# Gate and up chunks of the second block: one 512-column product for the high weights, and the two halves of a bank added on VectorE

## What is computed

```python
def swiglu(x, w_gate, w_up, w_down):
    return (jax.nn.silu(x @ w_gate) * (x @ w_up)) @ w_down

for l in range(DEPTH):                     # 2
    x = x + 0.5 * swiglu(rmsnorm(x, ffn1_norm[l]), ffn1_w_gate[l], ffn1_w_up[l], ffn1_w_down[l])
    x = x + hybrid_mixer(rmsnorm(x, mix_norm[l]), ...)
    x = x + 0.5 * swiglu(rmsnorm(x, ffn2_norm[l]), ffn2_w_gate[l], ffn2_w_up[l], ffn2_w_down[l])
```

## Time and profile before

| | before |
|---|---|
| median of 3 runs | 2207.34 us |
| the profiled execution: its own time, its span | 2209.08 us, 2207.3 us |
| TensorE busy, matmuls | 2139.0 us (97%), 17311 |
| VectorE busy | 1497.4 us (68%) |
| ScalarE busy | 1076.1 us (49%) |
| GpSimd busy | 581.6 us (26%) |
| mean DMA rate | 174 GB/s |

### The profile page before, as it was taken

One profiled execution on the slowest core, in us unless ns is written; L12 is line 12 of the kernel. 1 busy time (PEld: TensorE's weight loads), 2 busy tenths in 40 slices (PEclk: granted clock), 3 DMA queues, 4 the chain that ended last, 5 costly groups with the idle time before them and its releaser, 6 DMA issues.

```text
span 2207.3 us, 39976 instructions
## 1 busy us (share of the span) xinstructions
PE 2139.0 (97%) x17311; PEld 2033.7 (92%) x17311; DVE 1497.4 (68%) x1850; ACT 1076.1 (49%) x1432; POOL 581.6 (26%) x280
## 2 busy tenths in 40 slices
PE   7999999999999999999999999999999999999999
PEld 4989899898999888989999999889999999879999
DVE  5977775777678677676666556876556556786555
ACT  3666573433455747543345445554345444555433
POOL 0963315899248260466000000100000000100000
PEclk9999999999999999999999999999999999999999
DMA  9752346677657315566555555335555566434554
GB/s 317 235 170 85 111 127 193 228 261 234 206 169 228 107 39 160 175 197 221 183 191 172 191 191 172 112 99 177 187 191 171 192 191 191 132 98 142 187 189 133
DMA packets 332857, 383.95 MB, mean 174 GB/s; under 512 B 12551, under 2 KB 315402, under 8 KB 332554
## 3 DMA queue, kind: packets, MB, share of 16 engines
q1 hardware_dynamic: 332234, 381.23, 54.0%
q10 hardware_dynamic: 448, 0.16, 0.0%
HBM read 380.32 MB, written 1.05 MB: 173 GB/s over the span
## 4 chain that ended last, share of the span: by engine, by line
PE 74%; DVE 14%; ACT 7%; issue 3%; SPq 1%; DMA 0%; ACTq 0%; DVEq 0%
PE bank L761 16%; PE bank L762 16%; PE bank L763 15%; DVE weights_low L1457 6%; PE bank L1004 5%; PE bank L1003 5%; PE bank L1005 5%; ACT weights_high L2194 4%; DVE arena L1585 2%; PE bank L777 1%; PE bank L1042 1%; PE bank L1239 1%; PE bank L902 1%; PE bank L1224 1%; PE bank L894 1%
## 5 line engine op out<-in xcount | busy, mean ns | idle before, releaser
L1457 DVE TENSOR_TENSOR weights_low<-ring,weights_high 128x2048 fp32r<-128x2048 f32 (+1 forms) x304 | 752.2, 2474 | 429.0 <-ACT weights_high L2194 428.5
L761 PE MATMUL bank<-h_high,weights_high 128*128 128x256 f32 x3296 | 936.5, 284 | 22.6 <-DVE weights_low L1457 16.0
L762 PE MATMUL bank<-h_low,weights_high 128*128 128x256 f32 x3296 | 919.0, 279 | 0.0
L763 PE MATMUL bank<-h_high,weights_low 128*128 128x256 f32 x3296 | 915.8, 278 | 0.0
L2194 ACT ACTIVATE weights_high<-ring 128x2048 fp32r<-128x2048 f32 (+1 forms) x304 | 581.8, 1914 | 683.0 <-PE bank L763 530.2
L761 PEld LDWEIGHTS bank<-h_high,weights_high 128*128 128x128 f32 x3296 | 618.6, 188 | 43.2 <-DVE weights_low L1457 25.2
L762 PEld LDWEIGHTS bank<-h_low,weights_high 128*128 128x128 f32 x3296 | 620.3, 188 | 3.5 <-issue 3.4
L763 PEld LDWEIGHTS bank<-h_high,weights_low 128*128 128x128 f32 x3296 | 617.6, 187 | 0.0
L1003 PE MATMUL bank<-hidden_high,weights_high 128*128 128x256 f32 x1056 | 295.5, 280 | 1.8 <-DVE hidden_low L1723 1.0
L1004 PE MATMUL bank<-hidden_low,weights_high 128*128 128x256 f32 x1056 | 293.9, 278 | 0.0
L1005 PE MATMUL bank<-hidden_high,weights_low 128*128 128x256 f32 x1056 | 293.3, 278 | 0.0
(11 more groups left out here) (441 smaller groups left out, 2821.8 us busy)
## 6 DMA issues: line engine op xcount, KB each, us to landing
ring<-in_w_in SPq DMA_DIRECT2D x80, 1024.0 KB, 5.3
ring<-in_w_up SPq DMA_DIRECT2D x44, 1024.0 KB, 5.4
ring<-in_ffn_w_gate SPq DMA_DIRECT2D x44, 1024.0 KB, 5.4
ring<-in_ffn_w_up SPq DMA_DIRECT2D x44, 1024.0 KB, 5.4
ring<-in_ffn_w_down SPq DMA_DIRECT2D x44, 1024.0 KB, 5.0
side<-in_w_ada SPq DMA_DIRECT2D x42, 1024.0 KB, 7.9
ring<-in_w_down SPq DMA_DIRECT2D x22, 1024.0 KB, 5.0
ring<-in_w_dn_out SPq DMA_DIRECT2D x8, 1024.0 KB, 5.2
```

Source lines behind the costliest of these rows:

```text
L761: mm(o[:, m, :], a_, high[:, t, :], start=(t == 0), stop=False)
L762: mm(o[:, m, :], a_, low[:, t, :], start=False, stop=False)
L763: last = mm(o[:, m, :], b_, high[:, t, :], start=False, stop=(t == KT - 1))
L1457: v.tensor_tensor(low, wide(q), high.bitcast(F32), ALU.subtract).then_inc(chunk_split, 1)
```

## The change

`h_high` and `h_low` become the two halves of one tensor `h_both`, in the order and of the size they had. The gate and up chunks of the second block's four networks go through a new function `linear2`: for each half m and tile t, one product of the high weights with 512 columns (256 of the high input, then 256 of the low input), and one of the low weights with the high input, 256 columns, into the first 256 columns of the same bank. So each half m has a bank of its own: `L[...]` for m = 0, and `B[4]` or `B[5]` for m = 1. On VectorE `add_halves` sums each bank's two halves with one reduction (128 x 512 read, 128 x 256 written to SBUF); `rinv` and the hidden product then read SBUF. Two semaphores, `gate_added` and `up_added`, free the banks.

```diff
-        h_high = sb("h_high", P, KT, T, dt=F32R)
-        h_low = sb("h_low", P, KT, T, dt=F32R)
+        h_both = sb("h_both", P, 2, KT, T, dt=F32R)
+        h_high, h_low = h_both[:, 0], h_both[:, 1]
...
             if kind[0] == "g":
-                return gate_scaled, FP * (fi - 2) + i + 1
+                return gate_added, FP * (fi - 2) + i + 1
+            if kind[0] == "u" and fi >= 2:
+                return up_added, FP * (fi - 2) + i + 1
             return hidden_ready, FP * fi + i + 1
...
+        pair_bank = lambda key: (L[R[key] % 2], B[4 + R[key] % 2])
...
+            def linear2(key, norm=None):
+
+                n = SI[key]
+                wh, wl = WH[n % 2], WL[n % 2]
+                pe.wait_ge(chunk_split, n + 1)
+                pe.wait_ge(*release(PREV[key]))
+                for m in range(2):
+                    o = pair_bank(key)[m]
+                    both = o[:, :].rearrange("p (h t) -> p h t", h=2)
+                    for t in range(KT):
+                        if norm is not None and m == 0:
+                            pe.wait_ge(norm_ready, KT * norm + t + 1)
+                        a_, b_ = wh[:, t, m * P:(m + 1) * P], wl[:, t, m * P:(m + 1) * P]
+                        mm(both, a_, h_both[:, :, t, :], start=(t == 0), stop=(t == KT - 1), skip_group_check=True)
+                        last = mm(o[:, 0:T], b_, h_high[:, t, :], start=False, stop=(t == KT - 1), skip_group_check=True)
+                last.then_inc(chunk_multiplied, 1)
...
             def ffn(ka, kb, kc, l, ni, fi):
                 for i in range(FP + 1):
-                    if i < FP:
+                    if i < FP and ka != "ua":
+                        linear2((ka, l, i), norm=ni if i == 0 else None)
+                        if i == 0:
+                            sum_added(ni)
+                        linear2((kb, l, i))
+                    elif i < FP:
                         linear3((ka, l, i), h_high, h_low, norm=ni if i == 0 else None)
-                        if i == 0 and ni in ADDED:
-                            sum_added(ni)
                         linear3((kb, l, i), h_high, h_low)
...
+            def add_halves(key, dst):
+
+                return [v.tensor_reduce(dst[:, m * T:(m + 1) * T], b[:, :].rearrange("p (h t) -> p t h", h=2), AXX, ALU.add)
+                        for m, b in enumerate(pair_bank(key))]
+
             def hidden(key, fi, i, act, ahead):
 
-                dve.wait_ge(chunk_multiplied, M[key] + 1)
+                if fi < 2:
+                    dve.wait_ge(chunk_multiplied, M[key] + 1)
                 if i >= 2:
                     dve.wait_ge(hidden_ready, FP * fi + i - 1)
-                v.tensor_tensor(HT[:, i % 2, :], act, L[R[key] % 2][:, :], ALU.mult).then_inc(hid_whole, 1)
+                if fi < 2:
+                    v.tensor_tensor(HT[:, i % 2, :], act, L[R[key] % 2][:, :], ALU.mult).then_inc(hid_whole, 1)
+                else:
+                    v.tensor_tensor(HT[:, i % 2, :], act, FB[:, i % 2, :], ALU.mult).then_inc(hid_whole, 1)
...
-                    v.tensor_tensor(fa, LV[R[ka, l, i] % 2], over(rinv[:, :], 2), ALU.mult).then_inc(gate_scaled, 1)
+                    ins = add_halves((ka, l, i), FA[:, i % 2, :])
+                    ins[1].then_inc(gate_added, 1)
+                    then(ins[0])
+                    dve.wait_ge(gate_added, FP * (fi - 2) + i + 1)
+                    v.tensor_tensor(fa, fa, over(rinv[:, :], 2), ALU.mult).then_inc(gate_scaled, 1)
                     split(SI[kb, l, i] + 2)
                     dve.wait_ge(ffn_act, FP * fi + i + 1)
                     then(v.tensor_tensor(fa, fa, over(rinv[:, :], 2), ALU.mult))
+                    dve.wait_ge(chunk_multiplied, M[kb, l, i] + 1)
+                    ins = add_halves((kb, l, i), FB[:, i % 2, :])
+                    ins[1].then_inc(up_added, 1)
+                    then(ins[0])
+                    dve.wait_ge(up_added, FP * (fi - 2) + i + 1)
                     hidden((kb, l, i), fi, i, FA[:, i % 2, :], SI[kb, l, i] + (3 if i else 2))
```

More of the change, by code:

```diff
@@ L424, in build @@
         gate_scaled = sem("gate_scaled")
+        gate_added = sem("gate_added")
+        up_added = sem("up_added")
         squares_ready = sem("squares_ready")
```

## The result

| | before | after |
|---|---|---|
| median of 18 runs each | 2210.93 us (2205.24 to 2215.99) | 2215.82 us (2212.12 to 2220.19) |
| ratio after / before | | 1.0024 (95%: 1.0015 to 1.0032) |
| profiled execution | 2209.1 us, span 2207.3 | 2215.7 us, span 2213.9 |

The change makes the kernel 5 us slower: by the forecast's own bound of 0.5% no change, and outside the range that was given. A measured 0.2% can be told from nothing here only because there are 18 runs of each.

What follows compares the result with a forecast made beforehand. TensorE's pace bounds the kernel. Three networks at -2.41 us (-7.2) and the second at -3.8, heads included, give -11.0 us: 2198.1 from the profiled execution, 2196.3 from the median; range 2188 to 2213 for 8 in 10.

Steps and rivals of the forecast that it cites:

- the forecast's own bound: Whole kernel: a measurement can tell 0.5%, 11.0 us, from no change, so faster means below 2196.3 us.
- part 1: TensorE's gate and up chunks: three products become two, a pair takes 334.6 ns, 12.2 less, saving 0.193 us a chunk.
- 216 from 222: TensorE's product of 512 columns, in ns: 216 if the weight load hides, 222 if every handover costs 8.9.
- rival A: TensorE's pairs save little or nothing, the pace going with the columns; only the heads' loss remains, 2212.8 us; chance 0.14.
- Part 2: VectorE's sums: 176 reductions of 690 ns each, hidden in the idle time of steady turns, no delay.
- Rival B: VectorE's reductions cost double, 1.22 us, reading two halves 1 KB apart from PSUM; about 2230 us; chance 0.09.
- Part 3: Head of each network: sums delay u1 by 1.36 us, TensorE waits 2.1 us, net +1.26 us.
- D: TensorE's two paces are set anew after each wait: up to 4 us lost or 1 to 2 won; no own chance.
- C: TensorE's product of 512 takes 277 ns, each pair losing 46 ns; 2270 us; chance 0.03.

Runs made afterwards that it cites:

- experiment 7: The changed kernel without the product of the low weights with the high input, so products of 512 columns follow one another; 2130.98 us.
- experiments 9 and 10: Rounded weights of each gate and up chunk at its own place, 16-byte steps: 9 in the changed kernel, 2216.18 us; 10 in the kernel before, 2212.00 us.
- Experiments 3 and 4: Changed kernel: 3 leaves out the sums of the halves, 2210.42 us; 4 puts u1's weights ahead of the first hidden chunk at each head, 2208.63 us.
- experiment 5: The kernel before with u1's weights rounded and split ahead of the first hidden chunk; 2211.13 us beside 2209.01, ratio 1.0005.
- the scan: For triples: the kernel before with each gate and up chunk's rounded weights at its own place, in 16-byte steps; one run, 2212.00 us.

## Why the prediction was wrong

**The step that failed** is in part 1: "Nothing tells 216 from 222 ... I take the middle, 219." The product of 512 took 230 ns beside one of 256, and 226.7 by itself (experiment 7). At 116.5 for the small one the pair is 346.7 ns, so 0.193 us a chunk became 0. The prediction's own sign of being wrong, a pair outside 331 to 338 ns, came. The bounds held it: the high end was 231, and rival A stands on it.

Why the working led there: it looked for one rule for the loss, either by handover or by column, and took the plain products of the earlier trace rows as the nearest row. The experiments show neither. The loss of 768 columns goes from 20 to 46 ns with the place of the weights, for the same instructions (experiments 9 and 10), and the kernel before stood, in three of its four networks, where triples lose only 26.7. What an average triple loses couldn't be seen from one kernel; one sign was there and was used only to widen the range: two paces for the same work, which no loss by handover or by column explains. One sum of the prediction is off as well, without weight for the result: with 222 ns the forecast would be 7.5 us off (2199.8), not some 6 (2201).

The Trainium skill ("TensorE: Matmul & The Clock Gate", section "Wait — 56ns, not 53.3ns?") has about 2.5 ns as the fixed cost of a warm matmul. The product of 512 lost 13 to 17 ns here; the measurement decides against it, for fp32r operands, as it did for 256 columns.

**Part 2** held. 690 ns a reduction were forecast, 686 measured, and no wait appeared in the turns: the low weights still end 1.0 us ahead of TensorE. Rival B needed over 1.07 us. The Trainium skill ("SBUF — State Buffer", section "Door 1: The DMA port swizzle") says that any access pattern in PSUM that isn't contiguous slows matmuls down significantly. That is said of matmuls, and no run here shows it. For VectorE's reads rival B had no row: a reduction that takes its two elements 1 KB apart in a bank cost what one over neighbours in SBUF costs, 686 ns.

**Part 3** held, step by step. Counted from the start of the sum of the squares, 0.64 us earlier in this execution, gate x `rinv` was forecast at 1177.53 and came at 1177.59, the hidden product at 1182.39 and came at 1182.52, the low part of u1 at 1185.57 and came at 1185.72, u1's first product at 1187.91 and came at 1188.06. The wait is 1.58 us instead of 2.1, because TensorE reached it later than forecast: it had saved nothing on the way. The delay of u1 against before, 1.5 us a network, was forecast at 1.36. Experiments 3 and 4 show by two ways that it is the sums in VectorE's queue.

**The rivals.** A gave +5.4 us, from the head alone, with a chance of 0.14; measured +4.9. Its outcome came: a pair saves nothing at the kernel's places, and the heads are lost. Its reason, a pace that goes with the columns, is not what the runs show: the same 768 columns as a pair take 340.0 to 354.7 ns by place. That the size fits is in part luck: in the profiled executions the heads cost 6.0 us instead of 5.4, and the rest adds up to +0.6 only because its parts cancel. D came too, in another shape than it was told: the second network's gate and up chunks got the fast pace (-1.95 us) and the down chunks of the other three the slow one (+3.3), for chunks that the change doesn't touch. B and C didn't come.

**The range** ended at rival A's 2212.8. A's value against a base that is itself known to some 3 us (the three runs gave 2207.34, eighteen 2210.93) should have reached further: the same ratio on the first median is 2212.6, inside it.

**What stays open:** which bits of the two addresses matter, and whether it is the weights against the input, against each other, or both; why one place has two paces (346.7 and 350.0 to 351 ns for pairs, 346.7 and 353.3 for triples), which last for whole networks; and why the down chunk's pace goes against the gates' in some runs. Accumulation and the two runs of the input are excluded as the cause, each by one kernel. That VectorE and ScalarE work beside TensorE isn't it either, by the trace of before: in the first network a triple takes 346 to 347 ns while both are idle (18 triples) and while one or the other is busy throughout (216). Nothing here shows the mechanism. The runs of before, 2205 to 2216 us, may differ by such paces (a network at the slow one costs some 3 us, by experiment 5), but only one of them was profiled.

## What to carry to other kernels

Before a price from start to start is carried to another form of a product, vary the places of its operands by some tens of bytes: here that moved 768 fp32r columns between 340 and 366 ns, more than the change was about, and a tuned kernel may stand at a good place for its old form. Work put on an engine that idles is free only where its queue isn't on the path: the same 176 sums cost nothing in the turns and 6 us at four heads, and a swap of two steps took that back. When products get fewer and TensorE stays busy for as long, look at the pace of all its chunks, untouched ones too.

## What was not expected of the hardware

- The pace of fp32r products with the same shapes hangs on where the weights lie, in steps of 16 bytes over 256: pairs 340.0 to 354.7 ns, triples 340.0 to 366.0 (320.0 are columns).
- A place that is good for the pair isn't good for the triple, and the other way round: at (4, 4) 340.0 and 354.0 ns, at (12, 8), in one chunk each, 353.4 and 340.0.
- Neighbouring kinds of chunk trade paces: 5.554 + 5.547 + 5.652 and 5.600 + 5.600 + 5.547 us both make a turn of 16.75. Once in its turns, a network kept the one that it had for over 150 us.
- Held in all chunks, (12, 8) gave triples 353.3 ns in all but three, where the scan had 340.0: the place alone doesn't set the pace.
- A product of 512 fp32r columns in a row of its kind takes 226.7 ns, beside one of 256 it takes 230 and the small one 116.5.
